# Token tile 0 of the Pooling input product is made beside the rows of the first expert sum

## The reference, cut to what matters

```python
x = _post_norm(x, _peer(x * (1.0 + sc2) + sh2, *pw), g2, ...)   # layer 0: 128 experts per token
hx = x * (1.0 + sc1) + sh1                                        # layer 1
zg = (hx @ w_in).reshape(b, l, 4, 256)                            # Pooling's input product
pooled = stack(_centred_mean_minus_self(zg[:, :, g], (2, 4, 8, 16)[g]))   # along the tokens
y = einsum('blgc,gcd->blgd', pooled, w_grp).reshape(b, l, 1024) * scale @ w_out
```

## Time and profile before

| what | value |
|---|---|
| median of 3 runs | 2511.71 us (2511.37 to 2511.91) |
| profiled execution, its own time | 2511.54 us |
| its span, first to last instruction | 2509.7 us, 25967 instructions |
| busy share of the span | PE 91%, DVE 61%, PE weight load 61%, ACT 31%, POOL 23% |
| DMA | 776.49 MB, mean 309 GB/s; the gathers 536.90 MB, the panels 237.94 MB |
| the chain that ended last | DMA 25%, PE 17%, POOL 7%, DVE 6% of the span |
| mean granted PE clock | 0.993 of 2.4 GHz |

### The profile page before, as it was taken

How to read it: one execution, slowest core, us unless ns; L and a number is a source line. 1 busy time by engine, 2 the same in 40 slices (tenths; PEclk the granted TensorE clock), 3 DMA queues, 4 the chain that set the end, 5 groups by cost and what they waited for, 6 DMA issues and landing times.

```text
span 2509.7 us, 25967 instructions
## 1 busy us (share of the span) xinstructions
PE 2295.2 (91%) x8930; PEld 1518.6 (61%) x8930; DVE 1538.0 (61%) x3736; ACT 765.6 (31%) x2222; POOL 589.4 (23%) x529
## 2 busy tenths in 40 slices
PE   9999999999999999999999778777999998778777
PEld 8688888876888888585554323332775553233323
DVE  4854642256446323458777777776478767778774
ACT  2332100123230003334433333442244334233433
POOL 0000000000000000004445353443025454444432
PEclk9999999999999999999999999999999999999999
DMA  7315587353438754419999999999879999999997
GB/s 312 134 67 210 205 319 280 133 195 125 161 139 310 297 209 180 177 66 411 416 420 420 419 418 416 407 421 419 339 291 418 420 417 416 422 413 420 403 421 311
DMA packets 93043, 776.49 MB, mean 309 GB/s; under 512 B 10352, under 2 KB 11504, under 8 KB 12784
## 3 DMA queue, kind: packets, MB, share of 16 engines
q0 software_dynamic: 73728, 536.90, 51.8%
q1 hardware_dynamic: 19184, 237.94, 24.5%
HBM read 773.75 MB, written 1.05 MB: 309 GB/s over the span
## 4 chain that ended last, share of the span: by engine, by line
DMA 25%; PE 17%; POOL 7%; DVE 6%; issue 3%; ACT 2%; DVEq 0%; POOLq 0%; ACTq 0%
DMA arena<-tables,arena 15%; DMA weight_ring<-tables,arena 10%; PE misc L1960 7%; POOL arena L2159 4%; POOL weight_ring L2159 2%; DVE arena L2125 2%; PE tile L320 2%; PE tile L1848 2%; PE tile L333 2%; PE misc L1807 1%; DVE weight_ring L2125 1%; PE tile L348 1%; ACT arena L2072 0%; PE tile L2296 0%; PE tile L2297 0%
## 5 line engine op out<-in xcount | busy, mean ns | idle before, releaser
L1960 PE MATMUL misc<-arena 128*128 128x512 f32 x1328 | 635.9, 609 | 112.4 <-ACT arena L2072 111.8
L2159 POOL DMA_INDIRECT arena<-tables,arena x332 | 377.9, 1138 | 746.5 <-DVE arena L1326 345.5
L2125 DVE CUSTOM_DVE_ANT_0 arena<-arena,memT 128x1024 f32<-128x1024 f32 x332 | 404.7, 1224 | 186.7 <-DMA arena<-tables,arena 184.0
L1960 PEld LDWEIGHTS misc<-arena 128*128 128x128 f32 x1328 | 237.3, 193 | 394.6 <-issue 205.6
L1960 PE MATMUL misc<-weight_ring,arena 128*128 128x512 f32 x720 | 346.8, 617 | 87.1 <-ACT arena L2072 86.8
L320 PE MATMUL tile<-xT,weight_ring 128*128 128x256 f32 x1920 | 416.2, 379 | 0.0
L320 PEld LDWEIGHTS tile<-xT,weight_ring 128*128 128x128 f32 x1920 | 364.6, 190 | 51.2 <-issue 1.8
L1960 PEld LDWEIGHTS misc<-weight_ring,arena 128*128 128x128 f32 x720 | 130.5, 192 | 271.4 <-ACT arena L2072 146.9
L2125 DVE CUSTOM_DVE_ANT_0 weight_ring<-weight_ring,memT 128x1024 f32<-128x1024 f32 x180 | 220.2, 1225 | 120.5 <-DMA weight_ring<-tables,arena 119.7
L2058 ACT ACTIVATE arena<-arena 128x2 f32<-128x2 f32 (+1 forms) x262 | 53.3, 203 | 749.4 <-DVE arena L2125 749.1
L2159 POOL DMA_INDIRECT weight_ring<-tables,arena x180 | 205.8, 1143 | 135.4 <-DVE arena L1326 50.3
(11 more groups left out here) (393 smaller groups left out, 2419.7 us busy)
## 6 DMA issues: line engine op xcount, KB each, us to landing
weight_ring<-panels SPq DMA_DIRECT2D x103, 2048.0 KB, 8.6
arena<-panels SPq DMA_DIRECT2D x4, 2048.0 KB, 16.4
arena<-tables,arena POOLq DMA_INDIRECT x332, 12.8
weight_ring<-tables,arena POOLq DMA_INDIRECT x180, 17.5
arena<-c_rows SPq DMA_DIRECT2D x2, 1024.0 KB, 21.4
arena<-panels SPq DMA_DIRECT2D x2, 1024.0 KB, 8.5
weight_ring<-panels SPq DMA_DIRECT2D x1, 1536.0 KB, 10.8
cst<-consts SPq DMA_DIRECT2D x1, 1224.0 KB, 26.2
```

The source lines that it names most:

```text
L1960: ins = nc.tensor.matmul(M[2 * a + b][:, :], diag[:, s % NDIAG, :], slot(rows, s)[:, D + b * 512:D + (b + 1) * 512], start=first_row, stop ...
L2125: nc.vector.tensor_tensor_reduce(out=u, in0=u, in1=ht[:, n // PH, :], scale=1.0, scalar=0.0, op0=ALU.mult, op1=ALU.add, accum_out=dot[:, c ...
L2159: pool.indirect_dma_start(slot(rows, s), None, tables, bass.IndirectOffsetOnAxis(idx[:, n % 2, k:k + 1], 0)).then_inc(landing(rows, s), 16)
```

## The change

Both `pin` panels come early and the product of token tile 0 is made during the sum. From row 176 on, `Buffers` takes four far places (`LENT`: the two halves of ring slots 1 and 2) out of the queue; their last rows are then 174, 175, 163 and 164, and `rows_done` waits for these instead of row 252. Of far places four are left, so that only rows 236 to 239 must take far ones. In the new order, row 188 follows row 176, up to row 235 each follows the row 12 before it, 236 follows 228, 237 follows 229, 238 follows 234, 239 follows 235, 240 follows 224; rows 248 to 255 each follow the row 8 before.

PE makes two of the 64 products (128 columns) behind each of rows 216 to 247, into eight new tiles `pz`; ACT copies them to `early_z`, the scores of token tile 0, done with by then; POOL copies `early_z` into `zp` after the last row, behind its two memsets. DVE waits for that before the windows. After the sum PE makes only token tile 1, and ACT copies 128 columns per feature.

```diff
+PIN_ORDER = (4, 5, 6, 7, 0, 1, 2, 3)
...
+            + ([] if l else [("pz", i) for i in PIN_ORDER]))
...
+LENT = [("far", 2 * (BC_PANELS.index(("pin", i)) % SLOTS) + h) for i in (1, 0) for h in range(2)]
+GIVEN_BACK = 176
...
-            kind = ("near" if s >= HEADS * TOPK - HOME - RETIRED else "far") if s >= HEADS * TOPK - RING - RETIRED else None
+            far_rows = RING - HOME - (0 if l else len(LENT))
+            kind = (("near" if s >= HEADS * TOPK - HOME - RETIRED else "far")
+                    if s >= HEADS * TOPK - HOME - RETIRED - far_rows else None)
+            if l == 0 and s == GIVEN_BACK:
+                for place in LENT:
+                    queue.remove(place)
...
+        early_z = s12[:, 0, 0:KD * P].rearrange("p (f t) -> p f t", f=KD)
...
+            def early_pin(j, k):
+                f = PIN_ORDER[j]
+                if ("pin", f // 4) not in held:
+                    held["pin", f // 4] = e.panel("pin", f // 4)
+                if j == 0 and k == 0:
+                    pe.wait_ge(sem("hc_made"), KD)
+                bank = e.bank("pz", f) if k == 0 else T_[e.tiles.at("pz", f)[0]]
+                c = (f % 4 * KD + k) * P
+                ins = nc.tensor.matmul(bank[:, 0:P], held["pin", f // 4][:, c:c + P], hp[:, k, token_tile(0)],
+                                       start=(k == 0), stop=(k == KD - 1))
+                if k == KD - 1:
+                    e.filled(ins, "pz", f)
...
+                if l == 0 and 216 <= s < 248:
+                    for m in (2 * (s - 216), 2 * (s - 216) + 1):
+                        early_pin(m // KD, m % KD)
...
+                if l == 0 and s0 in range(222, 254, 4):
+                    f = PIN_ORDER[(s0 - 222) // 4]
+                    rd.free(nc.scalar.activation(early_z[:, f, :], rd.full("pz", f)[:, 0:P], ACT.Copy), "pz", f)
...
-                    if len(B_PANELS) <= j < len(B_PANELS) + SLOTS:
+                    if BC_PANELS[j][0] == "pin":
+                        sp.wait_ge(sem("row_used"), max(rows_b.last[("far", 2 * (j % SLOTS) + h)] for h in range(2)) + 1)
+                    elif len(B_PANELS) <= j < len(B_PANELS) + SLOTS:
...
-                e.several_tiles(e.panel("pin", 1), "pin", range(4, 8), KD, hp, T,
-                                last_ready)
-                w = e.panel("pin", 0)
+                late = hp[:, :, token_tile(1)]
+                e.several_tiles(held["pin", 1], "pin", range(4, 8), KD, late, P, last_ready)
                 for j in (2, 0):
-                    e.feature_tiles(w[:, j * KD * P:], "pin", j, 2, KD, hp, T)
+                    e.feature_tiles(held["pin", 0][:, j * KD * P:], "pin", j, 2, KD, late, P)
...
-                    rd.free(nc.scalar.activation(zp[:, f, PAD:PAD + T], rd.full("pin", f)[:, 0:T], ACT.Copy), "pin", f)
+                    rd.free(nc.scalar.activation(zp[:, f, PAD + P:PAD + T], rd.full("pin", f)[:, 0:P], ACT.Copy), "pin", f)
...
                 dve.wait_ge(sem("pad_set"), 2)
+                dve.wait_ge(sem("early_kept"), 1)
...
+                for f in PIN_ORDER:
+                    rd.read_wait("pz", f)
+                nc.gpsimd.tensor_copy(zp[:, :, PAD:PAD + P], early_z).then_inc(sem("early_kept"), 1)
```

More of the change, by code:

```diff
@@ L102, in peer_tiles @@
             + stage("ps", 4, 5, 6, 7, per=8) + stage("ht", 2, 3, per=4)
-            + stage("out", 0, 1, per=2) + stage("squares", 0, per=1) + stage("rows", 0, 1, 2, 3, per=4))
+            + stage("out", 0, 1, per=2) + stage("squares", 0, per=1) + stage("rows", 0, 1, 2, 3, per=4)
+            + ([] if l else [("pz", i) for i in PIN_ORDER]))
 BC_TILES = ([("zc", i) for i in (0, 2)] + [("zi", i) for i in range(6)] + [("uq", i) for i in range(12)] + [("kn", i) for i in range(8)]
@@ L1968, in peer_pe @@
             close_turn_pe(pe, l)
+            return held
         def peer_act(act, rd, l, beside_norm=None):
@@ L2352, in _ @@
                         values(j - 2)
-                peer_pe(e, rd, rows_b, 0, oxb, (lambda k: pe.wait_ge(sem("ox_read"), k + 1),), last_values)
+                held = peer_pe(e, rd, rows_b, 0, oxb, (lambda k: pe.wait_ge(sem("ox_read"), k + 1),), last_values)
                 def last_ready(k):
-                    if k == 0:
-                        pe.wait_ge(sem("hc_made"), KD)
                     pe.wait_ge(sem("close_dve" if k // 2 % 2 else "close_act"), 2 * (k // 4) + k % 2 + 1)
                 order = (4, 5, 6, 7, 2, 3, 0, 1)
-                e.several_tiles(e.panel("pin", 1), "pin", range(4, 8), KD, hp, T,
-                                last_ready)
-                w = e.panel("pin", 0)
+                late = hp[:, :, token_tile(1)]
+                e.several_tiles(held["pin", 1], "pin", range(4, 8), KD, late, P, last_ready)
                 for j in (2, 0):
-                    e.feature_tiles(w[:, j * KD * P:], "pin", j, 2, KD, hp, T)
+                    e.feature_tiles(held["pin", 0][:, j * KD * P:], "pin", j, 2, KD, late, P)
                 w = e.panel("grp", 0)
```

## The result

The changed kernel takes 2517.44 us (median of 12 runs, 2515.38 to 2518.68), the kernel before 2511.54 beside it (12 runs, 2510.59 to 2511.98). The ratio is 1.0023, 95% interval 1.0015 to 1.003: 5.9 us slower, inside the range that was given, and 1.7 us above the predicted time.

The account below looks back on a forecast made before the run. Bytes were taken to bound the kernel up to row 255, then a chain of engines. Panels + 10.0, buffers + 2.7, POOL's copy + 0.3 and tail - 9.0 gave + 4.0 us: 2515.5 us, range 2511.5 to 2520.0.

Parts of the forecast that it names:

- The bound: First expert sum and after: time is bytes up to row 255, then a chain of engines to the output product.
- The panels: Two panels moved from row 252 to row 175's use share busy DMA engines: cost 10.0 us.
- rival C: Ring and bytes cost less: row 238 not late, rows catch up 1.6 us; 2511.4 to 2513, chance 0.18.
- D: Panels hidden because dot, weight and matmul bound the rows: the 10.0 us vanish, 2505.7, chance 0.08.
- Four buffers fewer: Twelve row buffers from row 179: free except row 238 waiting for row 234, delaying 239 and 240; cost 2.7 us.
- B: Twelve buffers starve every head: rows 192, 208 and 224 each lose 2.7 us too; + 8.1, 2523.8, chance 0.10.
- PE, ACT, POOL in the rows: Early products and ACT copies beside rows 216 to 247 stay hidden while the clock is whole: cost nothing.
- POOL's copy: POOL's copy after the last row may hold DVE's two centring operations: 0.3 us taken, between 0 and 1.1.
- The tail: Half-width input product after the sum lets DVE start earlier and become the bound: gain 9.0 us.
- Rival A: PE's clock falls before the output product, costing 1.7 to 3.4 us: 2517.4 to 2519.1, chance 0.18.

Follow-up runs that it names:

- The panels alone: Kernel before with both panels early at row 176 and twelve buffers in natural order, input product still full width after the sum: 2521.12 us, ratio 1.004.
- the tail alone: Changed kernel with sixteen buffers, panels at row 252, nothing beside the rows; token tile 0's product left out, POOL sets zeros: 2502.28 us, ratio 0.9963.
- the panels one by one: Changed kernel with rows taking buffers in order, SP issuing the second panel only when the first has landed: 2512.01 us, ratio 1.0001.
- the buffers alone: Kernel before with only the changed kernel's buffers and their order; panels at row 252, product after the sum: 2515.25 us, ratio 1.0016.
- PE kept busy: Changed kernel with filler matmuls on PE in its three waits for DVE's windows: 2516.91 us, ratio 1.0018.
- three copies: Changed kernel with POOL's copy of token tile 0 made three times in a row, DVE's windows waiting for the third: 2517.20 us, ratio 1.0019.
- natural order: Changed kernel with no far rows kept for rows 232 to 239; each row up to 239 follows the row 12 before it: 2512.97 us, ratio 1.0005.
- only row 238 late: Kernel before with the changed kernel's buffers, but row 239 takes a buffer used 15 rows before: 2516.01 us, ratio 1.002.

## Why the prediction was right, and where a term was not

*The bound* was read rightly. Bytes set the pace up to row 255; after it the chain of engines does. The panels alone and the tail alone move the time by + 9.6 and - 9.2 us, as separate terms.

*The panels*, + 10.0: measured 9.86, and 9.83 alone. Nothing was caught up later, so the low end of 8.4 (rival C) is out, and so is D. What I said of the pattern was wrong: not ten rows 5 us apart, but two steps of 7.4 us one behind the other. Each is the time of the bytes of one row and one panel (3.15 MB at the 419 to 433 GB/s of the windows are 7.3 to 7.5 us). Equal shares of the engines for two panels and a gather would give 3 x 2.49 = 7.5 too, but a single early panel would then give steps of 5.0, and it gave one of 7.39. The sum didn't hang on this: with the panels one by one it was the same.

*Four buffers fewer*, + 2.7: this is the term that was mis-sized. Between the dots of rows 237 and 240 it measured 4.25 in the changed kernel, 3.21 in that with the buffers alone, and 4.5 by taking the order away. Two more profiles have the changed kernel's rows: with PE kept busy it was 3.70, with three copies 2.96. There more was lost a few rows on, so that from row 237 to row 255 the three are 4.39, 4.10 and 4.07 over before. The wait was found where it was put (POOL's issue of row 238 ended by PE), and row 238's own dot is late by 5.40 - 2.48 = 2.9, the 2.7 that was worked out. What failed is "rows 239 and 240 stand behind 238 on POOL and keep the delay". I priced one late row at the pace of a full queue for the next. But the queue had run empty, and refilled at 123 and 156 GB/s for two us, and row 239 is 1.3 us later still (0.2 to 1.1 in the other four profiles with this stall). Up to row 237 twelve buffers cost 0.03 us: B is out.

*PE, ACT, POOL in the rows*, nothing: right. PE works 40.24 of 46.00 us beside the early product at a clock of 1.00, and rows 190 to 237 keep their pace. The cover of a whole clock didn't last to the end: from 1745 to 1752, behind the stall, the granted clock was 0.54 beside the early product, and rows 240 to 255 took 0.14 us more in all.

*POOL's copy*, + 0.3: measured 0.11 (10.64 to 10.75 from the last dot to the input product, and 10.64 in the tail alone, where POOL only writes), since the copy met only the first 0.32 us of the centring. The rule of the Trainium skill (SBUF — State Buffer, Who interferes with whom), that the two kinds of instruction exclude each other, agrees with the three copies: the centring took 2.31 us instead of 1.42, and a copy that met it 1.38 instead of 1.04.

*The tail*, - 9.0: measured - 8.48 in the profiles of the changed kernel and of the panels one by one, both with the half clock, - 9.36 in natural order and - 9.47 alone. DVE's chain is 13.30 us for the 13.26 worked out, its start 7.75 us after the product's instead of 8.3.

*Rival A* was seen, in small: in the changed kernel's profile the clock fell to 0.51 for 3.4 us after PE's waits for DVE, and cost 1.5 us, not 1.7 to 3.4. It fell at the same place with the panels one by one and with three copies (2.08 us for the eight products in each), and not in natural order and in the tail alone, with the same waits of some 0.90 and 1.05 us ahead of it. It is of the size of the missing 1.7 us, as the late rows' extra 1.5 is, and the runs can't split the median between them: taking the order away gave 4.5, filling PE's waits 0.5 within the noise.

By the profiles + 9.86 + 0.03 + 4.25 + 0.14 - 8.48 + 0.18 = + 5.98, the medians' 5.9, against the predicted + 4.0.

## What to carry to other kernels

Where transfers set the pace, a panel moved ahead costs its bytes in full: here so for two at once, one after the other, one alone, and one ten rows later; move work into a gap behind the last transfer first (3.3 us here for no bytes) and pay bytes only for what still gains more than they cost. When buffers are taken away, write out for every row which use it waits for: one row that waited for the fourth before it cost what eighty rows on twelve buffers did not. Price such a stall by the first row's delay at least and by the time in which the queue is empty and refills at most (here 2.7 and 5.1, with 4.4 measured).

## What was not expected of the hardware

- The DMA engines, once empty, took two to three us of queued gathers until they moved their 420 GB/s again: 0, 82, 172 and 393 GB/s in four us one after the other with only row 238 late, 0, 123, 156 and 377 in the changed kernel.
- A dry spell of the DMA engines (98 GB/s at 1605) that was filled with other bytes came back 44 us later (205 GB/s at 1649), with no time gained.
- From 1589 to 1599 of the changed kernel, while PE waited for late rows, the granted clock was at 0.50, and nothing shows a price: rows 176 to 190 took no longer than the panels' bytes explain (+ 9.86 us for 4.19 MB).
